# Two fused transformer blocks on one core: retention merged with the latent projections, and the expert stage's first operands made in the spread stage

## The reference

```
h     = rms_norm(x, g_norm1) * (1 + sc1) + sh1          # sc, sh, gt from silu(c) @ w_ada
proj  = h @ w_in                                        # q_lat 256, kv_lat 128, k_rope 32, rq rk rv rg 512 each
y_mla : q  = rms_norm(q_lat) @ w_uq                     # 8 heads of 64 + 32, the 32 turned by rope
        kv = rms_norm(kv_lat) @ w_ukv                   # 8 heads of 64 + 64 (keys, values); k_rope turned, shared
        causal softmax attention
y_ret : retention with decay over rq, rk (rope), rv; per head (y - mean) * rsqrt(var); silu(rg) * y * gain
x     = x + gt1 * (concat(y_mla, y_ret) @ w_out)
h2    = rms_norm(x, g_norm2) * (1 + sc2) + sh2
PEER  : q = h2 @ w_query; for each of 8 heads the best 16 of 128 keys on either side, the best 16 of the
        256 pairs, gates = softmax;  expert = 128 * key1 + key2 of 16384
        out[t] = sum over the 128 picks of gate * gelu(expert_u[e] . h2[t]) * expert_v[e]
x     = rms_norm(x + gt2 * out, g_final)
```

## Time and profile before

| | us |
|---|---|
| median of 3 runs | 3002.99 |
| lowest, highest | 2993.77, 3009.70 |
| the profiled execution, its own time | 2994.3 |
| its span, first to last instruction | 2992.1 |
| TensorE busy in the span | 2700.6 (90%) |
| VectorE busy | 2110.3 (71%) |
| ScalarE busy | 1339.7 (45%) |
| GpSimd busy | 665.1 (22%) |

### The profile page before, as it was taken

How to read it: one execution, slowest core, us unless ns; L and a number is a source line. 1 busy time by engine, 2 the same in 40 slices (tenths; PEclk the granted TensorE clock), 3 DMA queues, 4 the chain that set the end, 5 groups by cost and what they waited for, 6 DMA issues and landing times. The chain is left out here.

```text
span 2992.1 us, 36195 instructions
## 1 busy us (share of the span) xinstructions
PE 2700.6 (90%) x12848; PEld 2214.6 (74%) x12848; DVE 2110.3 (71%) x3747; ACT 1339.7 (45%) x2070; POOL 665.1 (22%) x513
## 2 busy tenths in 40 slices
PE   4997889799869999999999987999889699999994
PEld 3664668457757899999999975866767588888883
DVE  4665558789857767777878776545634699999894
ACT  3224452226633333333333325443333488887883
POOL 2300013140033333334444421000000211222210
PEclk8998989899979999999999998999989799999997
DMA  7720011335489988888898943222230699999993
GB/s 227 275 73 18 1 59 57 120 116 210 191 317 336 326 287 289 288 288 303 306 314 297 314 169 87 101 85 78 94 113 10 215 408 378 369 371 373 368 356 122
DMA packets 266047, 651.64 MB, mean 218 GB/s; under 512 B 48293, under 2 KB 109477, under 8 KB 264617
## 3 DMA queue, kind: packets, MB, share of 16 engines
q1 hardware_dynamic: 219448, 507.13, 47.1%
q0 software_dynamic: 46448, 142.67, 14.4%
HBM read 617.09 MB, written 57.74 MB: 226 GB/s over the span
## 5 line engine op out<-in xcount | busy, mean ns | idle before, releaser
L3167 ACT ACTIVATE ex_w_hi<-expert_raw 128x1024 fp32r<-128x1024 f32 x384 | 373.8, 1073 | 36.3 <-PEq L94 15.6
L1890 PE MATMUL bank<-v_hi,peer_w_hi 128*128 128x512 f32 x768 | 300.9, 392 | 20.3 <-DVE peer_w_lo L1996 20.2
L3213 DVE TENSOR_TENSOR ex_w_lo<-expert_raw,ex_w_hi 128x1024 fp32r<-128x1024 f32 x256 | 296.0, 1218 | 8.3 <-ACT ex_w_hi L3167 7.1
L1890 PE MATMUL bank<-v_hi,peer_w_lo 128*128 128x512 f32 x768 | 300.7, 392 | 0.0
L1890 PE MATMUL bank<-v_lo,peer_w_hi 128*128 128x512 f32 x768 | 300.7, 392 | 0.0
L1932 ACT ACTIVATE v_hi<-v_in 128x1024 fp32r<-128x1024 f32 x128 | 130.3, 1054 | 332.2 <-PE bank L1890 298.1
L1878 PE MATMUL bank<-h_hi,u_hi 128*128 128x384 f32 x768 | 257.1, 335 | 0.2 <-DVE u_lo L1957 0.2
L1878 PE MATMUL bank<-h_hi,u_lo 128*128 128x384 f32 x768 | 257.1, 335 | 0.0
L1878 PE MATMUL bank<-h_lo,u_hi 128*128 128x384 f32 x768 | 256.9, 334 | 0.0
L1865 POOL DMA_INDIRECT got_rows<-in_u_rows,diff x128 | 182.9, 1429 | 313.7 <-DVE got_rows L1964 286.1
L1865 POOL DMA_INDIRECT got_rows<-in_expert_v,diff x128 | 182.0, 1422 | 249.0 <-DVE peer_acc L1969 208.5
(11 more groups left out here) (508 smaller groups left out, 6282.8 us busy)
## 6 DMA issues: line engine op xcount, KB each, us to landing
expert_raw<-in_w SPq DMA_DIRECT2D x384, 512.0 KB, 6.1
v_in<-in_expert_v SPq DMA_DIRECT2D x128, 512.0 KB
u_in<-in_u_tiles SPq DMA_DIRECT2D x96, 512.0 KB
ada_in<-in_w_ada SPq DMA_DIRECT2D x48, 512.0 KB, 5.1
gates_by_key<-spread SPq DMA_DIRECT2D x6, 4096.0 KB, 11.7
gate_in<-gates_by_key SPq DMA_DIRECT2D x384, 64.0 KB
ring<-in_w_in SPq DMA_DIRECT2D x11, 2048.0 KB, 8.3
early_u<-in_u_tiles SPq DMA_DIRECT2D x32, 512.0 KB, 3.8
```

Source lines behind the costliest of these rows:

```text
L1890: last = pe.matmul(g.bank[2 + o][:, :], x[:, par, e, i * P:(i + 1) * P], v[:, par, e, c], start=(first and n == 0), stop=(final and n == 3 ...
L3167: act.activation(hi[kind][:, c, :], raw_piece(raw, u * PIECES + c), ACT.Copy).then_inc(s["r_hi"], 1)
L3213: dve.tensor_tensor(lo[which][:, c, :], raw_piece(raw, u * PIECES + c), hi[which][:, c, :].bitcast(F32), ALU.subtract).then_inc(s["r_lo"], 1)
```

## The change

`retention` and the first stage of `latent_attention` become one stage, `mix_first`. The latents' squares and roots stand on ScalarE behind Silu, the inverse on VectorE in head 2, the scaling on ScalarE in heads 3 to 6; GpSimd turns `k_rope`. TensorE goes on from the last `sums` to the latents' transposes and to the same products in the same order as before; ScalarE's last roots of retention stand between its latent copies and its query copies. VectorE turns the queries in two halves, each behind four query copies. SyncE loads the weights at the stage's start. `decay`, `y_ret` and `sd` serve again as buffers.

`Opening` holds the buffers and semaphores that the spread and the expert stage share. In the spread stage SyncE loads the first two u tiles and the first two v tiles behind the second gate store; ScalarE makes the high parts of h (one in each of eight groups of the products) and of the two u tiles, VectorE the low parts after its last one-hot; SyncE loads the next two u tiles behind the last gate store. The stage no longer waits for the stores of the last gate block and of the early gelus; SyncE, GpSimd and (from step 1) ScalarE wait for them in the expert stage. TensorE's order there: transposes, up 16, up 17, down 0 to 15, then in a loop up q+2, down q, and down 62 and 63. High and low parts of u are made two steps ahead, gelus one step ahead, and the loads of u go out two steps ahead.

The diff, cut; TensorE's code of the latent products is moved as it stands, behind `sums(HEADS - 1)`:

```diff
+def mix_first(g, proj):
...
+        decay = ctx.enter_context(nc.sbuf_tensor("decay", [P, HEADS, T], F32))
+        y = ctx.enter_context(nc.sbuf_tensor("y_ret", [P, TT, BANK], F32))
+        early = ctx.enter_context(ExitStack())
...
+        kr_tmp = sb("kr_tmp", [P, 4, TT, ROPE // 2])
+        squares = y
+        lat, kt_mla = decay[:, 0:3, :], decay
...
+        turn_tmp = [sd[:, n // 2, n % 2 * 2:n % 2 * 2 + 2, :].rearrange("p b (x h w) -> p (b x) h w", h=HEADS, w=ROPE // 2) for n in range(4)]
...
+                sp.dma_start(gains[:, 0:2], a["g_q_norm"][0].rearrange("(k p) -> p k", p=P)).then_inc(s["d_w"], 16)
+                sp.dma_start(gains[:, 2:3], a["g_kv_norm"][0].rearrange("(k p) -> p k", p=P)).then_inc(s["d_w"], 16)
+                sp.dma_start(w_uq[:, :, :], a["w_uq"][0].rearrange("(k p) n -> p k n", p=P)).then_inc(s["d_w"], 16)
+                sp.dma_start(w_ukv[:, :], a["w_ukv"][0]).then_inc(s["d_w"], 16)
...
+                    if h == 2:
+                        dve.wait_ge(s["d_root"], 2)
+                        dve.reciprocal(lat_rs[:, :, :], lat_rms[:, :, :]).then_inc(s["d_rs"], 1)
                 center(dve, step, HEADS // 2 - 1)
                 close(dve, step, HEADS // 2 - 1)
+                dve.sem_inc(s["d_closed"], 1)
+                dve.wait_ge(s["d_kr"], 1)
+                kr = proj[:, :, C_KR:C_RQ]
+                step(dve.tensor_copy(kh[:, :, :, NOPE:QK], kr.unsqueeze(2).to_broadcast([P, TT, HEADS, ROPE])))
+                shape = [P, 2, HEADS, ROPE // 2]
+                for half in range(2):
...
+                    rotate(dve, step, qh[:, at, :, NOPE:NOPE + ROPE // 2], qh[:, at, :, NOPE + ROPE // 2:QK],
+                           few[0][:, at].unsqueeze(2).to_broadcast(shape), few[1][:, at].unsqueeze(2).to_broadcast(shape),
+                           [x[:, at] for x in turn_tmp])
+                dve.sem_inc(s["d_turned"], 1)
...
+                kr = proj[:, :, C_KR:C_RQ]
+                rotate(pool, InOrder(pool, s["d_pool"]), kr[:, :, 0:ROPE // 2], kr[:, :, ROPE // 2:ROPE], few[0], few[1],
+                       [kr_tmp[:, n] for n in range(4)])
+                pool.sem_inc(s["d_kr"], 1)
...
+                for i in range(TT):
+                    act.activation(squares[:, i, 0:Q_RANK], proj[:, i, C_QL:C_KV], ACT.Square, accum_out=lat_ss[:, 0, i:i + 1]).then_inc(s["d_sq"], 1)
+                    act.activation(squares[:, i, Q_RANK:C_KR], proj[:, i, C_KV:C_KR], ACT.Square, accum_out=lat_ss[:, 1, i:i + 1]).then_inc(s["d_sq"], 1)
+                act.wait_ge(s["d_sq"], 2 * TT)
+                act.activation(lat_rms[:, 0, :], lat_ss[:, 0, :], ACT.Sqrt, scale=1.0 / Q_RANK, bias=g.eps[:, :]).then_inc(s["d_root"], 1)
+                act.activation(lat_rms[:, 1, :], lat_ss[:, 1, :], ACT.Sqrt, scale=1.0 / KV_RANK, bias=g.eps[:, :]).then_inc(s["d_root"], 1)
+
+                def scale_latent(i):
+                    act.activation(proj[:, i, C_QL:C_KV], proj[:, i, C_QL:C_KV], ACT.Copy, scale=lat_rs[:, 0, i:i + 1]).then_inc(s["d_scaled"], 1)
+                    act.activation(proj[:, i, C_KV:C_KR], proj[:, i, C_KV:C_KR], ACT.Copy, scale=lat_rs[:, 1, i:i + 1]).then_inc(s["d_scaled"], 1)
...
+                    if h == 3:
+                        act.wait_ge(s["d_rs"], 1)
+                    if 3 <= h < 3 + TT:
+                        scale_latent(h - 3)
+                act.wait_ge(s["d_w"], 64)
+                for c in range(3):
+                    act.wait_ge(s["d_flipped"], c + 1)
+                    act.activation(lat[:, c, :], g.bank[c][:, :], ACT.Copy, scale=gains[:, c:c + 1]).then_inc(s["d_lat"], 1)
                 roots(HEADS // 2 - 1)
+                for n in range(8):
+                    i, half = n // 2, n % 2
+                    act.wait_ge(s["d_mm"], n + 1)
+                    act.activation(q_up[:, i, half * 384:(half + 1) * 384], g.bank[3 + n % 4][:, 0:384], ACT.Copy).then_inc(s["d_qk"], 1)
...
+                pe.wait_ge(s["d_scaled"], 2 * TT)
...
+        self.w = sb("peer_w", [P, KEYS_A_STEP, DENSE_T])
+        self.gates_stored = [g.nc.alloc_semaphore(f"gates_stored{i}") for i in range(2)]
+        self.gel_stored = [g.nc.alloc_semaphore(f"early_gel_stored{i}") for i in range(2)]
+        self.u_loaded = [g.nc.alloc_semaphore(f"first_ups{e}") for e in range(KEYS_A_STEP)]
+        self.v_loaded = [g.nc.alloc_semaphore(f"first_values{e}") for e in range(KEYS_A_STEP)]
...
+                for e in range(KEYS_A_STEP):
+                    dve.wait_ge(s["i_uhi"], e + 1)
+                    dve.tensor_tensor(opening.u_lo[:, e, :], opening.u_in[:, e, :], opening.u_hi[:, e, :].bitcast(F32), ALU.subtract).then_inc(s["i_ulo"], 1)
+                for k in range(DC):
+                    dve.wait_ge(s["i_hhi"], k + 1)
+                    dve.tensor_tensor(opening.h_lo[:, k, :], g.ht[:, k, 0:DENSE_T], opening.h_hi[:, k, :].bitcast(F32), ALU.subtract)
...
+                    if n % DC == 5 and n // DC < DC:
+                        k = n // DC
+                        act.activation(opening.h_hi[:, k, :], g.ht[:, k, 0:DENSE_T], ACT.Copy).then_inc(s["i_hhi"], 1)
+                    if n % DC == 5 and DC <= n // DC < DC + KEYS_A_STEP:
+                        e = n // DC - DC
+                        act.wait_ge(opening.u_loaded[e], 16)
+                        act.activation(opening.u_hi[:, e, :], opening.u_in[:, e, :], ACT.Copy).then_inc(s["i_uhi"], 1)
...
+                    if blk == 1:
+                        for e in range(KEYS_A_STEP):
+                            sp.dma_start(opening.u_in[:, e, :], g.a["u_tiles"][EARLY + e].rearrange("p c e -> p (c e)")).then_inc(opening.u_loaded[e], 16)
+                            sp.dma_start(opening.v_in[:, e, :], g.a["expert_v"][0, e * P:(e + 1) * P, :]).then_inc(opening.v_loaded[e], 16)
+                for e in range(KEYS_A_STEP):
+                    sp.wait_ge(s["i_ulo"], e + 1)
+                    sp.dma_start(opening.u_in[:, e, :], g.a["u_tiles"][EARLY + KEYS_A_STEP + e].rearrange("p c e -> p (c e)")).then_inc(opening.u_loaded[e], 16)
                 early.keep(sp, EARLY_SPREADING - 1)
-                early.saved(sp, EARLY_SPREADING)
...
-                    sp.wait_ge(stored[par], 16 * (NB // 2))
-
...
+                sp.wait_ge(stored[0], 16 * (NB // 2))
...
+            def last_gates(eng):
+                eng.wait_ge(opening.gates_stored[1], 16 * (NB // 2))
 
...
-                        if q > EQ:
-                            sp.wait_ge(s["j_ulo"], (q - EQ - 1) * GT + e + 1)
-                        sp.dma_start(u_in[:, e, :], a["u_tiles"][q * GT + e].rearrange("p c e -> p (c e)")).then_inc(s[f"j_u{e}"], 16)
+                        sp.wait_ge(s["j_ulo"], (q - EQ - 2) * GT + e + 1)
+                        sp.dma_start(u_in[:, e, :], a["u_tiles"][q * GT + e].rearrange("p c e -> p (c e)")).then_inc(opening.u_loaded[e], 16)
...
-                for q in range(Q):
+                for par in range(2):
+                    sp.wait_ge(opening.gel_stored[par], 16 * ((EARLY_SPREADING + 1 - par) // 2))
+                gel_ready(0)
+                last_gates(sp)
+                gates_in(0)
+                for q in range(1, Q):
                     down_in(q)
                     gates_in(q)
                     if q < EQ:
                         gel_ready(q)
-                    if EQ <= q + 1 < Q:
-                        up_in(q + 1)
+                    if EQ <= q < Q - AHEAD:
+                        up_in(q + AHEAD)
...
+            def up(pe, q, opens=False):
                 for e in range(GT):
-                    pe.wait_ge(s["j_ulo"], (q - EQ) * GT + e + 1)
-                    if reached(q, EQ + 1):
+                    if not opens:
+                        pe.wait_ge(s["j_ulo"], (q - EQ - 1) * GT + e + 1)
                         pe.wait_ge(s["j_gelu"], (q - EQ - 1) * GT + e + 1)
...
+                up(pe, EQ, True)
+                up(pe, EQ + 1)
                 pe.wait_ge(s["j_hrows"], 2)
-                for q in range(EQ - 1):
+                for q in range(EQ):
                     down(pe, q, q % 2, q == 0, False)
-                pe.wait_ge(s["j_hlo"], DC)
-                for q in (EQ, EQ + 1):
-                    up(pe, q)
-                    down(pe, q - 1, (q - 1) % 2, False, False)
-                with pe.Fori(EQ // 2 + 1, Q // 2) as it:
-                    up(pe, it * 2)
-                    down(pe, it * 2 - 1, 1, False, False)
-                    up(pe, it * 2 + 1)
+                with pe.Fori(EQ // 2, Q // 2 - 1) as it:
+                    up(pe, it * 2 + 2)
                     down(pe, it * 2, 0, False, False)
+                    up(pe, it * 2 + 3)
+                    down(pe, it * 2 + 1, 1, False, False)
+                down(pe, Q - 2, 0, False, False)
                 down(pe, Q - 1, 1, False, True)
...
             def act_u(act, q, e):
 
-                act.wait_ge(s[f"j_u{e}"], (q - EQ + 1) * 16)
```

(54 more changed lines are left out.)

490 lines of the change are left out of this document (220 added, 270 removed).

## The result

| | before | after |
|---|---|---|
| median of the paired runs | 3005.0 (7 runs) | 2981.6 (7 runs, 2968.1 to 2987.8) |
| profiled execution, its span | 2994.3, 2992.1 | 2985.5, 2983.7 |
| mean granted clock of that execution | 0.952 | 0.950 |

The ratio is 0.9929, with a 95% interval of 0.9912 to 0.9947: the kernel is 0.7% faster. The forecast was 2967, range 2952 to 2990. The time lies in the range, but 14 us above the forecast, and the change gave some 21 us by the ratio (23 by the medians) where 35.5 were summed.

The account below looks back on a forecast made before the run. TensorE was taken to bound the expert loop, with barriers and waits costing time in earlier stages. Merged stage 15.5 us plus opening 20 us gave 35.5 off the 3003.0 median: 2967.5, range 2952 to 2990.

Parts of the forecast that it names:

- The merged stage: Retention and latents: barrier and norm removed, queries turned in halves; 15.5 us gained, bounds 10.6 and 17.
- hole: TensorE's wait among the key and value groups, 2.17 us before, shrinks to some 0.4.
- half turns: Queries turned in 256-column halves at 0.45 us each, 2.7 us behind the last query copy instead of 4.4.
- rival 2: TensorE runs at 1.2 GHz after idling in merged stage and opening, losing up to 9 us: 2976.5; chance 0.12.
- The opening: Spread stage's end and expert stage's start: two up steps run before the first gates; 20 us gained, bounds 12 and 24.
- The four opening loads: Spread stage, SyncE's queue: four 0.5 MB loads ahead of later early_u loads cost nothing, up to 3 us if last.
- The first down product: Expert stage: starts at 849.5, bounds 847 and 853, after two up steps and the first gates.
- The sixteen steps: Down steps without up steps: transfers and TensorE even, 3 us of waits stay, next up step starts at 985.5.
- Rival 1: Transfers rule the opening: first down product at 853, sixteen steps at the transfers' pace; 2975.5, chance 0.22.
- rivals 1, 2 and 4: Said to give 23 to 27 us; the last has ScalarE late in the merged stage by 6 us: 2973.5, chance 0.07.
- The loop order: Expert loop: up running two steps ahead costs nothing, ScalarE and VectorE work staying under 16.5 us a pair.
- ScalarE in the merged stage: Retention sums: squares, roots and scalings moved to ScalarE are hidden, as it is busy 0.96 of 10 us.

Follow-up runs that it names:

- a_alone_1: The kernel before with the merged stage only, everything behind it as before; ratio to before 0.9944.
- before_one: The kernel before with one gathered row a step instead of two in the down steps ahead of the first up step; ratio to before 0.9960.
- b_alone_1: The kernel after with the old retention and latent stages, so the opening alone; ratio to before 0.9973.
- rows_one: Kernel after with opening loads spread behind early_u loads, last early gelus stored before second u pair, one gathered row a down step instead of two; ratio to before 0.9823.
- all_three: rows_one plus GpSimd's gathers held until first gates land, first u pair split early by GpSimd, second pair loaded before last gate store; ratio to before 0.9863.
- u_early: Kernel after with opening loads spread, gelus stored first, first u pair split early (low parts by GpSimd), second pair loaded before last gate store; ratio to before 0.9893.

## Why the prediction was right and wrong

**The merged stage (15.5 us): right.** M fell from 91.1 (three traces, 90.8 to 91.2) to 74.6 to 75.0 in three of eleven traces and 77.7 to 77.8 in eight: 16.3 or 13.3 us, on average 14.1. First query product (3.0 us against 3.3), hole, half turns and the rate of the second groups are as forecast. The 2.9 us between the two cases are rival 2's condition in the small: in a_alone_1 the clock is 0.50 in 240 to 245, and its query products take 12.94 us.

**The opening (20 us): wrong, a quarter of it came.** By the parts: L fell by 25.0 (24.9 forecast). The rest was mis-sized, and the sum fell below the lower bound of 12 that the prediction gave it.
- The four opening loads, "nothing, and up to 3 us if it is the last one", cost 8.7 of the 10.5 us by which S grew. The step was wrong in its argument: "a late early_u tile stops TensorE, which is not the pacer". TensorE had no lead on that tile (0.8 us of waiting in the trace before), and its banks and slots pass a longer wait on to VectorE. The transfers' share that I used came from 800 to 822, not from right behind a gate store, where a window of the kernel after (below) shows 393 GB/s at a share of 0.93. The check to make was the load's own landing: two more megabytes ahead of it at 393 GB/s are 5.3 us (it landed 6.3 later), and there was no slack.
- The first down product was put 30.5 us behind TensorE's end; it was 32.4. I counted the bytes ahead of the first gates, but not that SyncE may not even ask for them before the last gelus are stored, behind the u loads.
- The sixteen steps with what follows them were 136 us; from first down to first up product they took 141.3. "The change takes them out of that place" named eight low parts of h as the cause of the waits. They are gone, and the waits are not: the low parts were worth some 2 us (before_one). The transfers were the main cause; the same paragraph had them as even, 349 GB/s wanted, and 317 to 331 is what the kernel after got:

```profile
709.00:713.00 4.00, 4.00 (x27) 3.11 (x26) 4.00 (x14) 3.29 (x4) 0.00 (x0) 1.00 0.93 393
...
860.00:900.00 40.00, 39.49 (x173) 31.98 (x172) 30.25 (x45) 13.23 (x17) 14.03 (x10) 0.99 0.92 317
900.00:940.00 40.00, 37.18 (x162) 29.79 (x161) 30.73 (x47) 14.78 (x19) 13.07 (x9) 1.00 0.95 331
```

Rival 1 had the pace of the transfers, and forecast 2975.5 where 2981.6 was measured; it did not have the queue in the spread stage.

With these three sizes, 24.9 becomes 25.0 less 10.5, 2.7 and 8.5: 3.3 us, or 5 on the average of two traces on each side (before and a_alone_1, after and b_alone_1).

**The range: held, with luck.** 35.5 us were summed and some 19 are found in the stages. The time lies in the range because its upper end left room for the weaker cases and 9 us of spread, not because the mechanism of the opening was right. Two numbers of the prediction don't come out of its own terms either: with no waits and a first step at 847 the opening's upper bound is 26, not 24, and by their own times rivals 1, 2 and 4 give 26.5 to 29.5 us, not 23 to 27. Neither changes the forecast.

**The loop order (nothing): right.** L is 778.6 in all but two of the kernels with the new order (780.2 in those), also with 5.1 rows a step. **ScalarE in the merged stage (hidden): right**; the last sums end 43.4 and 43.5 us behind the issue of the gain load in the two profiles.

**The base.** The forecast kept the 8.7 us between before's profiled execution and its median. That distance was probably mostly the draw in attention: with the 83 us of most other traces instead of 75.9, before's profiled execution would have been near its median. No trace of a median execution of before was kept, so this is an estimate. Comparing the two profiles alone gives a gain of 8.8 us, of the medians 23.4. Neither number is that of the steps; the stages of the traces, 14.1 and 5, are nearest to them, and 19 us lies in the interval of the ratio (16 to 26).

## What to carry to other kernels

A load put into an issuing queue has to be priced at the next load behind it: look up when that one lands and how long its reader could have waited, not how busy the engines are on average. Where a stage runs at a DMA share of 0.95, take bytes out of it before looking for slow operations; here moving half a megabyte a step to steps with room was worth 10.7 us in those steps, for the change of one constant. And before a stage's length in one profile is compared, look at its granted clock in several.

## What the runs showed of the hardware

- TensorE's clock stayed at 1.2 GHz for 20 us while its records filled 19.54 of them; in rows_one and all_three the same products began at 2.4 GHz and never fell for long. Of fourteen executions eleven had such a stretch in attention, at its start in seven of eleven merged kernels and never there in the three with the old stage. What decides it was not found. Over the 140 timed runs of the fourteen kernels, fitted with one level for each kernel and one slope, 0.001 of mean granted clock goes with 2.1 us, and the scatter within a kernel falls from 5.9 us to 3.0: most of it goes with the clock.
- Beside GpSimd's 2.44 us subtraction VectorE lost 2.0 us in four one-hots (u_early).
- Right behind the issue of a 4.2 MB store the DMA engines moved 393 GB/s (709 to 713 of the kernel after); in the mixed traffic of the down steps 317 to 331 at a share of 0.92 to 0.95, where TensorE waited, and 287 to 292 at 0.89 to 0.90 in rows_one, where it did not.
